# Gate matrices of a product-key expert layer: one-hot products in one pass, with split gates

## The reference, cut to what matters

```python
def block(xb):                                   # per block of 128 tokens
    q = (xb @ peer_wq).reshape(128, 8, 2, 128)   # 8 heads, two half queries
    s = einsum('thpd,pkd->thpk', q, peer_subkeys)
    sv, si = top_k(s, 16)                        # 16 of 128 keys of each half
    ...                                          # the 16 best of the 256 pairs: experts i*128+j
    gate = softmax(fv)
    act = gelu(einsum('thkd,td->thk', peer_u[eidx], xb))
    return einsum('thk,thkd->td', gate * act, peer_v[eidx])
```

## Time and profile before

| | us |
|---|---|
| median of 3 runs | 4366.98 (4362.84 to 4368.19) |
| the profiled execution | 4355.38 |
| its span, first to last instruction | 4353.5 |
| the gate stage, from the first to the last product of the one-hots | 2173.0 to 2505 |

### The profile page before, as it was taken

One profiled execution on the slowest core, in us unless ns is written; L12 is line 12 of the kernel. 1 busy time (PEld: TensorE's weight loads), 2 busy tenths in 40 slices (PEclk: granted clock), 3 DMA queues, 4 the chain that ended last, 5 costly groups with the idle time before them and its releaser, 6 DMA issues.

```text
span 4353.5 us, 72544 instructions
## 1 busy us (share of the span) xinstructions
PE 4168.6 (96%) x27339; PEld 4038.6 (93%) x27339; DVE 2550.5 (59%) x4077; ACT 1342.7 (31%) x1857; POOL 746.7 (17%) x558
## 2 busy tenths in 40 slices
PE   7998979989899979999999999999999999999996
PEld 7998979989597979999999999999999999999996
DVE  4424233341212356666477746666679898898986
ACT  3332211231212132232355522222223333333333
POOL 1100020020000020024200011111123333344430
PEclk9999989989978999999999999999999999999998
DMA  7742222223431212233334489999999999999993
GB/s 199 215 114 59 78 65 78 70 66 116 169 141 49 77 50 78 82 118 121 122 134 161 168 310 354 356 350 356 355 328 403 409 398 405 391 399 398 401 390 134
DMA packets 557927, 943.08 MB, mean 217 GB/s; under 512 B 127060, under 2 KB 442128, under 8 KB 510280
## 3 DMA queue, kind: packets, MB, share of 16 engines
q1 hardware_dynamic: 504960, 567.36, 39.9%
q0 software_dynamic: 52848, 374.19, 21.4%
HBM read 866.63 MB, written 73.56 MB: 216 GB/s over the span
## 4 chain that ended last, share of the span: by engine, by line
PE 93%; DVE 3%; DMA 2%; ACT 1%; DVEq 1%; issue 0%; POOL 0%; SPq 0%; ACTq 0%
PE pp L194 28%; PE pl L1052 24%; PE pp L1111 12%; PE pl L1111 6%; PE pt L1111 6%; PE pp L1020 5%; PE pt L1029 2%; PE pp L971 2%; PE pp L936 1%; PE pp L955 1%; PE pp L822 1%; PE pt L928 1%; PE pl L983 1%; DMA p_f<-p_scr 1%; PE pl L784 1%; PE pt L786 1%
## 5 line engine op out<-in xcount | busy, mean ns | idle before, releaser
L1052 PE MATMUL pl<-h_hi,ut_hi 128*128 128x384 f32 x2048 | 734.7, 359 | 0.6 <-ACT ijt L1357 0.6
L1052 PE MATMUL pl<-h_hi,ut_lo 128*128 128x384 f32 x2048 | 692.2, 338 | 0.0
L1052 PE MATMUL pl<-h_lo,ut_hi 128*128 128x384 f32 x2048 | 691.3, 338 | 0.0
L1686 DVE TENSOR_TENSOR ut_lo<-pp,ut_hi 128x512 fp32r<-128x512 f32 x508 | 350.3, 690 | 482.4 <-ACT ut_hi L1310 481.6
L1310 ACT ACTIVATE ut_hi<-pp 128x512 fp32r<-128x512 f32 x508 | 304.2, 599 | 822.3 <-PE pp L1020 822.0
L209 DVE TENSOR_TENSOR w_lo<-raw,w_hi 128x2048 fp32r<-128x2048 f32 x120 | 274.7, 2291 | 363.5 <-ACT w_hi L204 363.5
L1382 ACT ACTIVATE v_hi<-v_raw 128x1024 fp32r<-128x1024 f32 x256 | 272.0, 1063 | 685.4 <-PE pl L1111 523.3
L1052 PEld LDWEIGHTS pl<-h_lo,ut_hi 128*128 128x128 f32 x2048 | 387.0, 189 | 0.0
L1052 PEld LDWEIGHTS pl<-h_hi,ut_hi 128*128 128x128 f32 x2048 | 386.2, 189 | 0.8 <-ACT ijt L1357 0.8
L1788 DVE TENSOR_TENSOR v_lo<-v_raw,v_hi 128x1024 fp32r<-128x1024 f32 x256 | 313.8, 1226 | 123.9 <-ACT v_hi L1382 123.0
L1052 PEld LDWEIGHTS pl<-h_hi,ut_lo 128*128 128x128 f32 x2048 | 384.7, 188 | 0.0
(11 more groups left out here) (342 smaller groups left out, 8574.6 us busy)
## 6 DMA issues: line engine op xcount, KB each, us to landing
u_raw<-in_peer_u SPq DMA_DIRECT2D x256, 512.0 KB, 5.1
v_raw<-in_peer_v SPq DMA_DIRECT2D x256, 512.0 KB, 7.7
p_f<-p_scr SPq DMA_DIRECT2D x256, 192.0 KB, 10.2
raw<-in_w_in SPq DMA_DIRECT2D x24, 1024.0 KB, 5.6
g_scr<-gs POOLq DMA_DIRECT2D x6, 4096.0 KB, 12.9
raw<-in_w_mk SPq DMA_DIRECT2D x16, 1024.0 KB, 5.8
raw<-in_w_mv SPq DMA_DIRECT2D x16, 1024.0 KB, 5.8
raw<-in_w_out SPq DMA_DIRECT2D x16, 1024.0 KB, 5.8
```

Of the source, the lines that this page charges most:

```text
L1052: last = mm(pl[:, d, 0:N], w[:, d, k, :], x[:, k, S:S + N], start=(k == 0 and w is ut_hi and x is h_hi), stop=(k == KC - 1 and w is ut_lo))
L1686: tt(ut_lo[:, d, 4 * g:4 * g + 4, :], src.rearrange("p (c i) -> p c i", c=4), ut_hi[:, d, 4 * g:4 * g + 4, :].bitcast(F32), ALU.subtract). ...
```

## The change

- The gate is split into hi and lo (ght), as other operands are. The one-hot of i times the gate becomes oh_i, with two halves side by side: one-hot times hi and one-hot times lo, 256 columns. The one-hot of j (oh_j) is the stationary operand. Both are float32r, so that a product of four tokens is four matmuls of 256 columns (line 1028 of the changed kernel). It fills two banks: pt (now one tensor pt2 of two banks) for even groups, pp[1] for odd ones.
- The transposed rows have only the two banks of pp[0] in this stage (pair_bank), so a bank of transposes waits for the rows_lo of two groups before, not of four.
- The one-hots are made on three engines. ACT makes oh_j: four Abs of 128 elements (|k - j|, with the number j as a bias from SBUF), and a Relu of 1 - x over 512. DVE makes the one-hot of i for four tokens in one tensor_tensor of 512 and multiplies it by the gates' hi in a second. POOL multiplies it by lo.
- On the way out ACT copies the hi half into gs (gate_hi_out), one group later than before, and DVE adds the lo half to it there (gate_out).
- The stage is written out without loops. At its end PE waits for the last gate_out and the last rows_lo; before, PE waited for the last copy only after all 128 columns.
- Some semaphores are merged. POOL's stores stand between its products.

```diff
+        def gate_bank(s):
+            return pt2 if s == 0 else pp[1]
+        def pair_bank(g):
+            return pp[0][:, g % 2, :]
...
         def turn_rows(i, d, g, dst, first=False, two=False):
-                    pe.wait_ge(t_lo, i * 8 + (4 * d + g - 3))
+                    pe.wait_ge(t_lo, i * 8 + (4 * d + g - (1 if two else 3)))
...
+            def gate_matrix(n):
+                s = n % 2
+                pe.wait_ge(act_gate, 5 * (n + 1) + max(0, n - 1))
                 pe.wait_ge(oh_ready, n + 1)
+                if n >= 2:
                     pe.wait_ge(g_out, n - 1)
                 for x in range(4):
-                    last = mm(pt[s][:, x * P:(x + 1) * P], oh[:, s, 0, x, :], oh[:, s, 1, x, :], ...)
+                    last = mm(gate_bank(s)[:, x // 2, x % 2 * 2 * P:(x % 2 + 1) * 2 * P], oh_j[:, s, x, :],
+                              oh_i[:, s, x, :, :].rearrange("p h i -> p (h i)"), start=True, stop=True)
                 last.then_inc(g_done, 1)
...
-            gate_columns(pe, column)
+            gate_columns(column)
+            pe.wait_ge(g_out, 16 * 2 * ND)
+            pe.wait_ge(t_lo, 4 * (PICK + 8 * ND + 1))
...
+            def gate_hi_out(n):                                             # ACT
+                act.wait_ge(g_done, n + 1)
+                f(gs[:, n // 16 % 2, :, t0:t0 + 4].rearrange("p i t -> p t i"), both[:, :, 0, :], ACT.Copy)\
+                    .then_inc(act_gate, 1)
+            def one_hot_j(n):                                               # ACT
+                if n >= 2:
+                    act.wait_ge(g_done, n - 1)
+                for x in range(4):
+                    f(oh_jf[:, s, x, :], iota_k[:, :], ACT.Abs, bias=ijt[:, 1, 4 * n + x:4 * n + x + 1]).then_inc(act_gate, 1)
+                act.wait_ge(act_gate, 5 * n + 4 + max(0, n - 1))
+                f(oh_j[:, s, :, :], oh_jf[:, s, :, :], ACT.Relu, bias=one, scale=-1.0).then_inc(act_gate, 1)
...
+                    if gate is not None:                                    # ACT, column, group g
+                        one_hot_j(4 * gate + g)
                     if more:
+                        rows_hi(...)
+                    if gate is not None and 4 * gate + g >= 1:
+                        gate_hi_out(4 * gate + g - 1)
                 gelu(i, d)
...
+            def gate_column(i, d, gate):                                    # DVE
                 for g in range(4):
+                    n = 4 * gate + g
+                    gate_times_hi(n)                # waits for POOL's product of group n
+                    if n + 1 < 32 * ND:
+                        one_hot_i(n + 1)            # waits for g_done of group n - 1
+                    rows_lo(i + d, 1 - d, g, pair_bank(g))
+                    if n >= 1:
+                        gate_out(n - 1)             # waits for gate_hi_out(n - 1)
```

More of the change, by code:

```diff
@@ L119, in program @@
         pp = [ctx.enter_context(nc.psum_tensor(f"pp{i}", [P, 2, 512], F32)) for i in range(2)]
[L120 removed]
+        pt2 = ctx.enter_context(nc.psum_tensor("pt", [P, 2, 512], F32))
+        pt = [pt2[:, i, :] for i in range(2)]
         pl = ctx.enter_context(nc.psum_tensor("pl", [P, 2, 512], F32))
@@ L531, in program, with gate_columns @@
         NSTEP = 2 * (NS + P)
[L533 to L550, removed]
+        def gate_columns(column):
+            for n in range(8 * ND):
+                column(PICK // 2 + n // 2, n % 2, n)
+        def gate_bank(s):
+            return pt2 if s == 0 else pp[1]
+        def pair_bank(g):
+            return pp[0][:, g % 2, :]
         @block.sync
@@ L1008, in _, with turn_rows @@
                     select_scores(i * 2 + (WQ0 + d - 1), (d + 1) % 2)
-            def turn_rows(i, d, g, dst, first=False):
+            def turn_rows(i, d, g, dst, first=False, two=False):
                 if g % 2 == 0:
@@ L1057, in column @@
                         if more:
-                            turn_rows(i + d, 1 - d, k // 4, turn_bank(k // 4))
+                            turn_rows(i + d, 1 - d, k // 4, (turn_bank if gate is None else pair_bank)(k // 4),
+                                      two=gate is not None)
                         if gate is not None:
-                            gate_matrix(group(gate, k // 4)[0], k // 4 % 2)
+                            gate_matrix(4 * gate + k // 4)
                 if isinstance(i, int) and 1 <= 2 * i + d <= 8:
@@ L1320, in column @@
                 for g in range(4):
+                    if gate is not None:
+                        one_hot_j(4 * gate + g)
                     if more:
[L1322 to L1329, removed]
+                        rows_hi(i + d, 1 - d, g, (turn_bank if gate is None else pair_bank)(g),
+                                None if first or g else i * 2 + d)
+                    if gate is not None and 4 * gate + g >= 1:
+                        gate_hi_out(4 * gate + g - 1)
                 gelu(i, d)
@@ L1356, in _ @@
                 act.wait_ge(ijt_done, x + 1)
-                f(ijt[:, x, :], pt[0][:, 0:N], ACT.Copy).then_inc(ijt_out, 1)
-            gate_columns(act, column)
+                dst = (ijt[:, 0, :], ijt[:, 1, :], ght[:, 0, :])[x]
+                f(dst, pt[0][:, 0:N], ACT.Copy, scale=-1.0 if x == 1 else 1.0).then_inc(ijt_out, 1)
+            act.wait_ge(ijt_out, 3)
+            gate_columns(column)
+            gate_hi_out(32 * ND - 1)
             with act.Fori(PICK // 2 + 4 * ND, GELU_S) as i:
@@ L1728, in _, with one_hot_i @@
             dve.wait_ge(ijt_out, 3)
-            def one_hot(n, s, t0):
-                if not (isinstance(n, int) and n < 2):
+            tt(ght[:, 1, :], pt[0][:, 0:N], ght[:, 0, :].bitcast(F32), ALU.subtract).then_inc(ght_lo, 1)
+            def one_hot_i(n):
+                if n >= 2:
                     dve.wait_ge(g_done, n - 1)
[L1733 to L1737, removed]
+                tt(oh_if[:, n % 2, :, 0, :], iota_k[:, :].rearrange("p (x k) -> p x k", x=1).to_broadcast([P, 4, P]),
+                   ijt[:, 0, 4 * n:4 * n + 4].rearrange("p (x k) -> p x k", k=1).to_broadcast([P, 4, P]),
+                   ALU.is_equal).then_inc(ohi_eq, 1)
@@ L1747, in _ @@
+                    if n >= 1:
+                        gate_out(n - 1)
+            one_hot_i(0)
+            gate_columns(gate_column)
+            gate_out(32 * ND - 1)
             done = [0]
```

90 lines of the change are left out of this document (55 added, 35 removed).

## The result

The changed kernel takes 4386.49 us, median of 5 runs (4381.51 to 4392.43). The kernel before took 4365.88 in the runs beside them (4362.84 to 4368.19). The medians lie 20.6 us apart. The ratio over all runs is 1.0053, 95% interval 1.0042 to 1.0063: some 18 to 27 us slower. The forecast was 4382, its own range 4374 to 4392.

What follows compares the result with a forecast made beforehand. PE bound the old kernel; ACT would bound the changed gate stage. Stage 10.8, drain 2.9, half clock 1.5 and start 0.3 gave +15.5 us on the 4366.98 median: 4382, own range 4374 to 4392, wider range 4345 to 4410.

Steps and rivals of the forecast that it cites:

- PE stops being the bound, ACT and DVE set the group: Gate stage: ACT's sum 3.374 us a group, DVE's loop 3.41, PE's 3.03; PE idle 0.4 to 0.5 a group.
- PE's own group of 3.03: Gate stage, PE's work per group: matmuls 2.11, transposes 0.44, four gate products 0.48 us; 0.43 less than before.
- ACT's prices: Gate stage, ACT per group: Abs 0.392 us each, Relu 0.713, copy into gs 1.103; sum 3.374 after overlaps.
- GELU: Once a column on ACT: 0.385 us, plus 0.43 waiting for the column's last matmul.
- DVE's loop: Gate stage: copies, gate_out, product with hi, then PE's part; 6.81 us for two groups, 3.41 each.
- the Trainium skill's larger figure: gate_out on DVE with the hop in gs: 1.44 us by the skill's rates, about 8 us more in total.
- Drain: End of the gate stage: PE waits for the last gate_out, +2.9 us.
- Half clock behind it: After the stall at the stage's end: lower PE clock slows nine matmuls by 0.16 us each, +1.5 us.
- rival 1: Gate stage: PE stays the bound, kernel faster at 4330 us; chance 0.09, wholly or in part.
- ACT cheaper than forecast: Gate stage: free pointers cut ACT's sum to 2.88 us, DVE's loop stays; 4368 us, no change; chance 0.17.
- gate_out paying twice: DVE in gate stage: hop paid on read and write, 1.70 us, or POOL slows DVE; 4410 us; chance 0.20.
- The clock did not fall in the stage: Rival claim denied here: PE's gaps lower the clock in the gate stage, 4400 us or more; 0.04 with others.

## Why the prediction was right, point by point

**PE stops being the bound, ACT and DVE set the group.** Right, and shown from both sides: taking work from ACT alone or from DVE alone gave 0.8 and 0.45 us a column at most, while the two reliefs at once with the GELU out of the way gave 2.7 and brought PE back to its own 3.02. PE's idle time is 40.3 us over 96 groups, 0.42 each, where 0.4 to 0.5 was forecast, and it is released by ACT's Relu and by DVE's product with hi, as forecast.

**PE's own group of 3.03.** Right: 3.02 in the two kernels with the reduction and the late GELU. The 0.70 to 0.74 that the chain gives a gate product for which PE had waited is no higher price: it runs from the first one's start to the last one's end, and is 0.72 in the kernel that never waits, too. To the next matmul's start it is 0.55 in the mean, where 0.51 was put.

**ACT's prices.** Right: Abs 0.393 (0.392), Relu 0.724 (0.713), copy into gs 1.11 (1.103), and a sum of 3.32 (3.374) where ACT is the bound.

**GELU.** 0.385 and a wait of 0.43 were forecast; the group with the GELU is 0.74 longer than the others, and moving it was worth 0.8 us a column (14.52 to 13.71).

**DVE's loop, 3.41 forecast.** This is the term that was mis-sized. gate_out was put at 1.19 and took 1.37. The loop over two groups became 7.02 instead of 6.81 (ut_hi starts at 2311.80 and, two groups later, at 2318.82). gate_out takes 0.10 more of it (1.29, from 2313.45 to the start of the product with hi at 2314.74, since that starts 0.08 before gate_out's end), the hand-over from DVE to PE 0.06 more (0.10 for 0.04), PE's part 0.05 more (3.31 for 3.26). Thus DVE's loop, not ACT's 3.37, set three groups of four: 3 x (3.51 - 3.374) = 0.41 of the 0.49 us by which a column (14.80) is longer than the forecast's 14.31. That is the sentence "longer gate_out goes straight into the time". Some of it was a slip of the sum: my own figure for DVE's loop, 3.41, was above the 3.374 that I summed with, and three groups of four by it would have been 2.6 us more. The bounds (0.69 to 1.70) held gate_out; no run here has the hop on the read or on the write alone, so which of them the 0.18 belongs to stays open.

The stage cost 19.6 us, forecast 10.8. The 0.49 a column would be 11.8 us more, but I had also put the column of before too short: from the start of the first to the start of the last gate products lie 23.75 columns and 330.9 us, so it was 13.93 and not 13.86, which takes 1.7 off; the other 1.3 is that the changed stage also has 23.75 of its columns, and shorter groups at both ends. It is longer than the 340 to 346 us that I had named as a sign. By the 8 us that I added for the Trainium skill's larger figure (1.44 us) the forecast would have been 4390, 3.5 above the measured time; by mine it was 4.5 below. Those 8 us were themselves too few: 0.25 us more in the loop make it 3.53 a group, which over three groups of four is 11.

**Ends of the stage.** Start 0.3 forecast, 0.3 measured. Drain 2.9 forecast, 3.17 measured. Half clock behind it 1.5 forecast: the matmuls there start 0.32 apart instead of 0.17 and the whole end costs 4.7 against 4.4 forecast, 1.6 beyond the stall. The clock fell in six of the nine kernels with a stall here, this one among them, and not in one with a stall of the same length, so that the term came true was partly luck.

**Sum.** +15.5 forecast. By the medians it is +20.6 (18 to 27), and the parts of the traces that are the change's give 0.3 + 19.6 + 4.7 = 24.6, inside that interval. Against this the forecast was 9 us short, nearly all of it in the stage. The lower edge of the range, 4345, isn't half way to rival 1 as said (that would be 4356); the time lies far from either.

**The rivals.** PE as the bound, and ACT cheaper than forecast, are excluded by the waits and the prices above. gate_out paying twice happened in part: 1.37 of 1.70. The clock did not fall in the stage.

## What to carry to other kernels

When work moves off the engine that sets the time, write down each other engine's loop for one group, from a tile's release to the next wait for it, and not only its sum of busy time: here DVE was 86% busy and still set three groups of four. An instruction that needs the very end of the bound engine's work must not stand in the middle of a stream that feeds this engine; moved behind the next feed it left PE without a wait, once ACT had the time. If two engines are a little too slow, relieving one gives a small part of what both give together (0.45 or 0.8 us a column here, against 2.7).

## What the runs showed of the hardware

- A tile written with a hop of 256 bytes after each element cost ACT 1.11 us for 512 elements against 0.59 without. The DVE add that reads and writes it took 1.37 against 0.68.
- A DVE reduction that reads 1024 elements from PSUM and writes 512 with that same hop took 1.22, and 512 elements of a tensor_tensor without a hop 0.68 to 0.69. From 512 to 2560 elements without a hop an element costs 1.04 ns, so 1024 would take about 1.22 by estimate: the hop is not seen when one element is written for two read. The Trainium skill, "Vector Engine (DVE) Microarchitecture Reference", section 5.2, reports the full read rate for an operation whose one read stream alternates between two regions and that writes one word for two read. The trace agrees, with the read in PSUM, and here the write hops as well.
- Four products of 256 columns, at a clock of 1.00, start 0.20 and then 0.12 and 0.12 apart, whether their operands were long there (the kernel with reduction and late GELU) or had just come (the first step is 0.19 to 0.23 in the changed kernel, but for the first product of all). From the first one's start to the next matmul's it is 0.56 in the one and 0.55 in the mean of the other.
- A DVE product of two SBUF tensors that starts while a POOL instruction reads SBUF waits for it in full but for the last 0.13 us of POOL's record: 109 products in two kernels, with 0.27 to 1.29 us of the record to come.
- After stalls of PE of 1.97 to 3.17 us the granted clock was 0.5 for some three us in six kernels and stayed at 1.00 in two, one of them with 3.17; after 1.39 it stayed at 1.00.
